# Ranking the product keys inside the routing stage: a PEER layer on one Trainium2 core

## The reference: what is computed

```python
sc = jnp.einsum('thcd,hcnd->thcn', q, keys)          # 8 heads, 2 halves, 128 keys
v1, i1 = lax.top_k(sc[:, :, 0], 16)                  # first level
v2, i2 = lax.top_k(sc[:, :, 1], 16)
cand = (v1[..., :, None] + v2[..., None, :]).reshape(t, 8, 256)
best, ci = lax.top_k(cand, 16)                       # second level
e = take(i1, ci // 16) * 128 + take(i2, ci % 16)
g = softmax(best)
out = sum_k gelu(x . u[e_k]) * g_k * v[e_k]
```

## Time and profile before

| | before |
|---|---|
| median of three runs | 3452.57 us (3450.69 to 3453.32) |
| the profiled execution, its own time | 3452.24 us |
| its span, first to last instruction | 3450.1 us |
| mean granted TensorE clock | 0.966 |
| TensorE matmul busy | 3190.7 us, 92% |
| VectorE busy | 2307.2 us, 67% |
| the 32 items of query and scores | about 820 to 1019 us |
| `hidden` | about 1019 to 2334 us |

### The profile page before, as it was taken

How to read it: one execution, slowest core, us unless ns; L and a number is a source line. 1 busy time by engine, 2 the same in 40 slices (tenths; PEclk the granted TensorE clock), 3 DMA queues, 4 the chain that set the end, 5 groups by cost and what they waited for, 6 DMA issues and landing times. The chain is left out here.

```text
span 3450.1 us, 45082 instructions
## 1 busy us (share of the span) xinstructions
PE 3190.7 (92%) x17090; PEld 2873.6 (83%) x17090; DVE 2307.2 (67%) x4358; ACT 995.5 (29%) x1127; POOL 1662.2 (48%) x847
## 2 busy tenths in 40 slices
PE   7988678988989999999999999994999999999998
PEld 5776578877879999999999999993788888888886
DVE  2510678822118789999899999883676666666665
ACT  3211347722112223333333333331122212112110
POOL 2510010022203564555454545664878777777773
PEclk9999789999999999999999999997999999999999
DMA  3242552141224676676666666888887787787784
GB/s 131 89 167 83 144 107 47 29 165 67 92 62 138 212 235 205 226 249 232 240 233 236 229 243 233 288 314 317 303 311 281 286 303 273 288 305 275 288 295 154
DMA packets 262430, 722.32 MB, mean 209 GB/s; under 512 B 22000, under 2 KB 88432, under 8 KB 255088
## 3 DMA queue, kind: packets, MB, share of 16 engines
q1 hardware_dynamic: 188528, 451.52, 38.6%
q0 software_dynamic: 73728, 268.47, 22.1%
HBM read 581.50 MB, written 138.41 MB: 209 GB/s over the span
## 5 line engine op out<-in xcount | busy, mean ns | idle before, releaser
L1188 PE MATMUL hid_ps<-side_hi,u_hi 128*128 128x384 f32 x2048 | 533.1, 341 | 23.5 <-POOL u_lo L874 16.9
L883 POOL DMA_INDIRECT found<-in_u,pick_u x232 | 333.3, 1437 | 420.1 <-DVE found L1119 386.8
L1188 PE MATMUL hid_ps<-side_lo,u_hi 128*128 128x384 f32 x2048 | 524.1, 337 | 0.0
L1188 PE MATMUL hid_ps<-side_hi,u_lo 128*128 128x384 f32 x2048 | 523.8, 336 | 0.0
L1920 PE MATMUL part<-v_hi,act_hi 128*128 128x512 f32 x1536 | 476.4, 392 | 48.5 <-POOL act_lo L1843 48.3
L1920 PE MATMUL part<-v_lo,act_hi 128*128 128x512 f32 x1536 | 475.4, 391 | 0.0
L1920 PE MATMUL part<-v_hi,act_lo 128*128 128x512 f32 x1536 | 474.9, 391 | 0.0
L874 POOL TENSOR_TENSOR u_lo<-u_raw,u_hi 128x1024 fp32r<-128x1024 f32 x128 | 330.3, 2580 | 267.9 <-ACT u_hi L833 267.3
L1859 DVE TENSOR_TENSOR acc<-acc,part 128x1024 f32<-128x1024 f32 x192 | 234.4, 1221 | 319.8 <-PE part L1920 319.6
L1188 PEld LDWEIGHTS hid_ps<-side_hi,u_hi 128*128 128x128 f32 x2048 | 368.0, 190 | 24.2 <-issue 12.7
L1838 POOL TENSOR_TENSOR v_lo<-v_raw,v_hi 128x2048 fp32r<-128x2048 f32 x64 | 295.8, 4621 | 183.8 <-ACT v_hi L1811 183.2
(11 more groups left out here) (204 smaller groups left out, 5148.3 us busy)
## 6 DMA issues: line engine op xcount, KB each, us to landing
u_raw<-in_uT SPq DMA_DIRECT2D x128, 512.0 KB, 3.6
v_raw<-in_v SPq DMA_DIRECT2D x64, 1024.0 KB, 6.9
hid_d<-hid SPq DMA_DIRECT2D x128, 384.0 KB, 3.4
gate_d<-stage SPq DMA_DIRECT2D x48, 1024.0 KB, 6.1
act_in<-hid_d SPq DMA_DIRECT2D x64, 768.0 KB, 6.6
gate_in<-gate_d SPq DMA_DIRECT2D x32, 1536.0 KB, 14.5
w_raw<-in_w_in SPq DMA_DIRECT2D x6, 2048.0 KB, 8.3
k_hi<-k_hi_d SPq DMA_DIRECT2D x32, 256.0 KB, 8.1
```

Of the source, the lines that this page charges most:

```text
L883: pool.indirect_dma_start(found[:, g], None, u_d, bass.IndirectOffsetOnAxis(ap=pick_u[:, g, n:n + 1], axis=0))\
L1188: mm = pe.matmul(hid_ps[:, s % 2, half, 0:W], w[:, s % 2, ch], x[:, ch, GB * P + half * W:GB * P + (half + 1) * W], start=n == 0, stop=n = ...
```

## The change

The five steps on the 16 score rows leave `hidden` and run in `route`, item by item, on the four token blocks of an item. VectorE reads the scores from PSUM where it copied them before. Of an item only the 16 values and the 16 places of each token are stored, in two DMAs, to two new tensors in memory; `hidden` loads these (two DMAs of 128 KB for a token block instead of one of 1 MB). TensorE now waits with the scores of item `n` until the best eight of item `n - 2` are taken out (`rest_ok`). In `hidden` the remaining steps of `rank` are spread over 16 slots anew, and the DMA, the exponentials and the counts of the semaphore `ranked` move with them.

```diff
@@ route, SP
-                sp.wait_ge(sc_sb, n + 1)
-                sp.dma_start(score_d[4 * half:4 * half + 4, :, key * NK:(key + 1) * NK]
-                             .rearrange("b t n -> t b n"), sc[:, n % 2]).then_inc(sc_out[n % 2], 16)
+                sp.wait_ge(top_ok, n + 1)
+                for out_d, kept in ((top_d, top), (top_ix_d, top_ix)):
+                    sp.dma_start(out_d[4 * half:4 * half + 4, :, key * K:(key + 1) * K]
+                                 .rearrange("b t n -> t b n"), kept[:, n % 2]).then_inc(top_out[n % 2], 16)
@@ route, VectorE
-            for n in range(SCORED):
-                dve.wait_ge(sc_ok, n + 1)
+            def reached(semaphore, value, step):
+                dve.wait_ge(semaphore, value)
+                dve.memset(tick[:, step:step + 1], 0.0)
+
+            def first_values(n):
                 if n >= 2:
-                    dve.wait_ge(sc_out[n % 2], 16 * (n // 2))
-                dve.tensor_copy(sc[:, n % 2], sc_ps[:, n % 2]).then_inc(sc_sb, 1)
+                    dve.wait_ge(top_out[n % 2], 32 * (n // 2))
+                reached(sc_ok, n + 1, 0)
+                for b in range(4):
+                    last = dve.max(top[:, n % 2, b, 0:8], sc_ps[:, n % 2, b])
+                last.then_inc(first_ok, 1)
+
+            def first_indices(n):
+                reached(first_ok, n + 1, 1)
+                for b in range(4):
+                    dve.max_index(top_ix[:, n % 2, b, 0:8], top[:, n % 2, b, 0:8], sc_ps[:, n % 2, b])
+                for b in range(4):
+                    last = dve.match_replace(rest[:, n % 2, b], top[:, n % 2, b, 0:8], sc_ps[:, n % 2, b], LOW)
+                last.then_inc(rest_ok, 1)
+
+            def second_values(n):
+                reached(rest_ok, n + 1, 2)
+                for b in range(4):
+                    last = dve.max(top[:, n % 2, b, 8:16], rest[:, n % 2, b])
+                last.then_inc(second_ok, 1)
+
+            def second_indices(n):
+                reached(second_ok, n + 1, 3)
+                for b in range(4):
+                    last = dve.max_index(top_ix[:, n % 2, b, 8:16], top[:, n % 2, b, 8:16], rest[:, n % 2, b])
+                last.then_inc(top_ok, 1)
+
+            for n in range(SCORED + 1):
+                if n < SCORED:
+                    first_values(n)
+                if n >= 1:
+                    second_values(n - 1)
+                if n < SCORED:
+                    first_indices(n)
+                if n >= 1:
+                    second_indices(n - 1)
@@ route, TensorE
-                    pe.wait_ge(sc_sb, n - 1)
+                    pe.wait_ge(rest_ok, n - 1)
@@ hidden, SP
-            def load_scores(tb):
-                sp.dma_start(score[:, :, :], score_d[bass.ds(tb, 1)]...).then_inc(score_in, 16)
+            def load_tops(tb):
+                for kept, in_d in ((top, top_d), (top_ix, top_ix_d)):
+                    sp.dma_start(kept[:, :, :, :].rearrange("p h c k -> p (h c) k"),
+                                 in_d[bass.ds(tb, 1)].rearrange("o t (n k) -> t (o n) k", k=K)).then_inc(top_in, 16)
...
-                    if phase == 0 and s == 7:
+                    if phase == 0 and s == 4:
@@ hidden, ScalarE
-                    if phase == 0 and s == 6:
+                    if phase == 0 and s == 2:
                         exponents(0)
-                    if s == (14 if phase == 0 else 12) and not last:
+                    if s == (12 if phase == 0 else 9) and not last:
                         exponents(tb + 1)
@@ hidden, VectorE: the keys_* steps are gone; rank(tb, s) is now
+   s 0 pair_sums, 1 pairs_first_values, 3 pairs_first_indices, 4 pairs_take_out, 6 pairs_second,
+   7 pairs_second_indices, 8 split_picks, 9 look_equal 0, 10 look_times 0, 11 look_sum 0,
+   12 look_equal 1, 13 look_times 1, 14 look_sum 1 and sum_shares
```

More of the change, by code:

```diff
@@ L386, in _, with route @@
                         last.then_inc(qt_ok, 1)
-def route(nc, a_hi, a_lo, x_first, ident, x_d, w_out_d, norm_g_d, wq_d, keysT_d, h_d, score_d):
+def route(nc, a_hi, a_lo, x_first, ident, x_d, w_out_d, norm_g_d, wq_d, keysT_d, h_d, top_d, top_ix_d):
     G = 6
@@ L415, in route @@
         qT = xs[:, 0].rearrange("p (s n) -> p s n", s=2)
-        sc = xs[:, 1].rearrange("p (s b n) -> p s b n", s=2, b=4)
+        rest = xs[:, 1].rearrange("p (s b n) -> p s b n", s=2, b=4)
+        tops = gain.rearrange("p (x s b k) -> p x s b k", x=8, s=2, b=4)
+        top = tops[:, 0]
+        top_ix = tops[:, 1].bitcast(U32)
+        tick = sb("tick3", [P, 4])
         ss = sb("ss3", [P, TB])
@@ L445, in route @@
         sc_ok = sem("sc_ok")
-        sc_sb = sem("sc_sb")
-        sc_out = [sem("sc_out0"), sem("sc_out1")]
+        first_ok = sem("first_ok3")
+        rest_ok = sem("rest_ok3")
+        second_ok = sem("second_ok3")
+        top_ok = sem("top_ok3")
+        top_out = [sem("top_out0"), sem("top_out1")]
         block = c.enter_context(nc.Block())
@@ L663, in _, with hidden @@
                     score_item(n - 1)
-def hidden(nc, x_hi, x_lo, x_first, iota, iota16, ident, uT_d, u_d, score_d, hid_d, gate_d, pick_v, pick_act,
+def hidden(nc, x_hi, x_lo, x_first, iota, iota16, ident, uT_d, u_d, top_d, top_ix_d, hid_d, gate_d, pick_v, pick_act,
            blocks=TB):
@@ L685, in hidden @@
     PARTS = 4
-    RANKS = 13
+    RANKS = 8
     LOOKS = 8
@@ L825, in exponents @@
             def exponents(tb):
-                act.wait_ge(ranked, RANKS * tb + 10)
+                act.wait_ge(ranked, RANKS * tb + 5)
                 act.activation(share[:, :, :], share[:, :, :], ACT.Exp).then_inc(exped, 1)
@@ L915, in _ @@
         def _(dve):
-            streams = [(h, half) for h in range(H) for half in range(2)]
             def gate_factors(tb, s, early):
@@ L939, in reached @@
                 dve.memset(tick[:, :], 0.0)
[L943 to L972, removed]
             def pair_sums(tb):
-                reached(ranked, RANKS * tb + 5)
+                dve.wait_ge(top_in, 32 * (tb + 1))
                 dve.tensor_copy(top_ixf[:, :, :, :], top_ix[:, :, :, :])
@@ L984, in pairs_first_values @@
             def pairs_first_values(tb):
-                reached(ranked, RANKS * tb + 6)
+                reached(ranked, RANKS * tb + 1)
                 for h in range(H):
@@ L990, in pairs_first_indices @@
             def pairs_first_indices(tb):
-                reached(ranked, RANKS * tb + 7)
+                reached(ranked, RANKS * tb + 2)
                 for h in range(H):
@@ L996, in pairs_take_out @@
             def pairs_take_out(tb):
-                reached(ranked, RANKS * tb + 8)
+                reached(ranked, RANKS * tb + 3)
                 for h in range(H):
@@ L1002, in pairs_second @@
             def pairs_second(tb):
-                reached(ranked, RANKS * tb + 9)
+                reached(ranked, RANKS * tb + 4)
                 for h in range(H):
@@ L1017, in split_picks @@
             def split_picks(tb):
-                dve.wait_ge(ranked, RANKS * tb + 11)
+                dve.wait_ge(ranked, RANKS * tb + 6)
                 dve.tensor_scalar(pick_part[:, 0], pick[:, :, :], 4, None, ALU.logical_shift_right)
                 dve.tensor_scalar(pick_part[:, 1], pick[:, :, :], 15, None, ALU.bitwise_and).then_inc(ranked, 1)
-                dve.wait_ge(ranked, RANKS * tb + 12)
+                dve.wait_ge(ranked, RANKS * tb + 7)
                 dve.tensor_copy(pick_partf[:, :, :, :], pick_part[:, :, :, :]).then_inc(ranked, 1)
@@ L1039, in look_equal @@
                 else:
-                    dve.wait_ge(ranked, RANKS * tb + 13)
+                    dve.wait_ge(ranked, RANKS * tb + 8)
                 dve.tensor_tensor(cand[:, :, :, :], pick_partf[:, half].unsqueeze(3).to_broadcast([P, H, K, K]),
@@ L1069, in rank @@
                 if s == 0:
[L1070 removed]
+                    pair_sums(tb)
                 if s == 1:
[L1072 to L1074 removed]
+                    pairs_first_values(tb)
                 if s == 3:
[L1076 removed]
+                    pairs_first_indices(tb)
                 if s == 4:
[L1078 to L1080 removed]
+                    pairs_take_out(tb)
                 if s == 6:
[L1082 removed]
+                    pairs_second(tb)
                 if s == 7:
[L1084 removed]
+                    pairs_second_indices(tb)
                 if s == 8:
[L1086 removed]
+                    split_picks(tb)
                 if s == 9:
[L1088 removed]
+                    look_equal(tb, 0)
                 if s == 10:
[L1090 to L1091 removed]
+                    look_times(tb, 0)
                 if s == 11:
[L1093 removed]
+                    look_sum(tb, 0)
                 if s == 12:
[L1095 to L1096 removed]
+                    look_equal(tb, 1)
                 if s == 13:
[L1098 removed]
                     look_times(tb, 1)
@@ L1977, in layer @@
             x_first = sb("x_first", [P, GB, D])
```

(4 more changed lines are left out.)

18 lines of the change are left out of this document (8 added, 10 removed).

## The result

The changed kernel takes 3458.36 us (median of nine runs, 3454.32 to 3467.87) against 3450.11 us of the kernel before beside it: a ratio of 1.0027 with an interval of 1.0018 to 1.0036, about 8 us slower. The forecast was 3497 us in a range from 3468 to 3548: the sign was right, the size wrong by a factor of five.

A forecast was written before the change was run, and what follows sets the result against it. TensorE bounds query and scores; TensorE and VectorE are both full in blocks 2 to 7 of hidden. Route +71, weight loads +10, hidden -36 gave +45 on 3452.24: 3497 us, range 3468 to 3548.

The forecast's parts named there:

- the price of an item: In route: an item takes 8.3 us instead of 6.35, 5.4 of VectorE work plus 2.9 waiting for stores; +71 us with the tail.
- the gain in `hidden`: Blocks 2 to 7 of hidden: TensorE no longer waits for VectorE's ranking; 36 us gained, bounds 20 to 42.
- The round trip: In route's loop: VectorE stands still each item until two stores land; 2.9 us, from 2.4 to 4.5.
- rival (b): Stores in route: short pieces cost much more, 4.5 us or above a trip, items 9.9 or more; 3547 us and up; 13%.
- VectorE's work: In route: twenty ranking operations an item replace one copy; 5.4 us (5.0 to 5.8), 0.4 of it for reading PSUM.
- The weight loads: In route: weight loads queued behind later stores hold back ScalarE's query copy; 5 us, twice, +10 us (6 to 16).
- the turns of the loop: In hidden: three turns cost about 7 us each beyond a slot; these 21 us stay.
- a further part: In hidden: waits go only in part, as steps of 2.3 to 3.3 us fall on single slots; low bound 20 us.
- the smaller load is on no path: In hidden: loading two of 128 KB instead of one of 1 MB changes the time by 0.
- rival (c): In route: TensorE's clock falls because it waits about 2 us in every 8.3; +36 us, 3533; 10%.
- (a): In route: the round trip isn't in the loop, TensorE keeps its pace and the kernel gains; 3423 us; 5%.
- (d): hidden gives little, as gathers or the port shared with GpSimd hold the slots: 8 us instead of 36, 3525; 10%.

## Why the prediction was wrong

**The mechanism in `route` was right, and the size fell above all with one term: the price of an item.** I put it at 8.3 us, and it is 7.26; 30 items make 31 us of that. Both of its parts were too high. A second term, the gain in `hidden`, was 9 us too low.

- The round trip, 2.9 us: measured 2.38. The second issue comes 0.42 us behind the first (0.44 taken), SP starts 0.03 us after VectorE ends (0.05 taken), but a store lands in 1.9 and not 2.3 us. I took the row of stores of 512 pieces of 512 bytes, since the count of pieces was the same. The runs bracket it: 2.3 at 512 pieces of 512 bytes, 1.8 at 512 of 128, 1.9 at 512 of 64, 1.5 at 128 of 256. A quarter of the count is worth 0.4 us, and so is an eighth of the bytes, and the small loads at 1.7 to 2.2 were the nearer row (64 KB each, and not an eighth of a MB, as I wrote). Stores in short pieces landed no later than the one in pieces of 512 bytes, so rival (b) is refuted. The Trainium skill ("DMA: Bandwidth & Descriptors", Specifications) says that the engines read, modify and write below 512 bytes; whether they did so here no run shows, but a price of rival (b)'s size on the landing isn't there.
- VectorE's work, 5.4 us: measured 4.88. The 0.4 us for reading PSUM isn't there. The groups by line of the changed kernel, columns as in the page's part 5, put the same operation out of PSUM (L615, L621) beside the one out of SBUF (L629, L635):

```profile
L621 DVE FIND_INDEX8 gain<-gain,sc_ps 128x8 uint32<-128x128 f32 x128 | 34.7, 289 | 0.0
...
L635 DVE FIND_INDEX8 gain<-gain,xs 128x8 uint32<-128x128 f32 x128 | 34.1, 284 | 0.0
L615 DVE MAX8 gain<-sc_ps 128x8 f32<-128x128 f32 x128 | 28.3, 283 | 93.3 <-issue 77.6 <-PE sc_ps L689 15.7
L629 DVE MAX8 gain<-xs 128x8 f32<-128x128 f32 x128 | 27.8, 279 | 0.0
```

  The difference is 4 to 5 ns an operation. The row of copies had said 0, and the sum should have gone by it instead of by half the length of a copy. The Trainium skill ("VectorE: DVE Perf Modes", section on the TRN2 errata), by which I had estimated 65 ns, isn't borne out for these operations. The four waits cost 0.2 us in all, and not 0.3.

**The weight loads**, 5 us each: measured 6.2. Chain and place were as forecast. With the early loads the 13 us waits of TensorE are gone, so the late loads were the cause.

**hidden**, 36 us: measured 45.4, above the high bound of 42. The bound went by a floor in which the turns of the loop kept their 21 us above a slot. That step failed: the turns fell by 6.7 us, and without them the gain is 38.7, inside my bounds. Why they fell is open. I had set a further part aside for steps that fall on single slots. There was next to no such loss, for the change also lays the steps out anew and spreads the look-up steps one to a slot; with the old slots 21 us of the gain are lost, a term that my sum had not named. My statement that the smaller load is on no path is neither shown nor refuted.

**TensorE.** I forecast waits of 2 us in each item and a rival (c) in which they cost clock. TensorE made no such waits: it is behind VectorE after each weight load and never far ahead.

With the measured terms the forecast's own sum comes out: 45 - 31 + 2.4 (loads) - 9.4 (hidden) = +7, the 7.2 us between the two shifts. The range missed because I cut off its low corner. An item at 7.4 and hidden at 42 gave +7 to +11 by my own bounds, 3459 to 3463 us, and I ended the range at 3468 although the low end of an item rested on rows and its high end on a guess.

That the sign came out right is in part luck. It hung on 7 us between 52.6 lost and 45.4 gained: an item 0.25 us shorter, a quarter of the error that I made in it, would have left nothing of them; with one store, at 6.72 us an item, the kernel is no slower than before (0.9984 to 1.0003). My 0.91 for slower was too sure.

**Rivals.** (a), no round trip in the loop, is refuted for this kernel; with four places the trip is out of the loop, and with early weights too the kernel takes 3418 us. (b), dear short pieces, and (d), little from `hidden`, are refuted. (c), a falling clock, didn't occur: the clock is 1.00 in the steady items.

## What to carry to other kernels

When work is moved into a loop that already stores its results, look at which store the first write of an iteration waits for: with two places and a software pipeline of depth two that is the one just issued, and its whole round trip stands in the loop. Four places took it out; three, which by the order of the steps should do, weren't tried. And when a loop that also orders prefetches gets longer, the prefetches come later by the same order: move them ahead with it. Spread the steps of a planned side job so that no slot has more than the slack of its buffers; the mean load alone doesn't tell.

## What the runs showed of the hardware

MAX8, FIND_INDEX8 and MATCH_REPLACE8 on 128 columns follow one another at 0.20 to 0.27 us whether they read PSUM or SBUF. A store of 32 KB lands 1.5 us after its issue in 128 pieces and 1.9 us in 512. An issue of such a store on SP takes 0.3 to 0.5 us as a rule, and in some items up to 1.9. In the profile a wait of VectorE for a DMA can carry the name "issue"; the landing times of SP's issues tell what it was. After a wait of 13.18 us TensorE took 2.08 us for scores that take it 1.05 otherwise; a wait of 1.93 us stands before a group of 3.07 us in one trace, and one of 1.88 had none of that effect in the kernel before, so the length of the wait alone doesn't settle it. That stays open.
